# Two unused buffers in front of the h buffers and of the weight slots of a hybrid attention layer

## The reference

```python
x  = x + sincos_2d(rows, GRID_W, d)
m  = (silu(c) @ w_ada + b_ada).reshape(9, d)          # shift, scale, gate of each sub-layer; mc from c_ctx
# 1: half-step SwiGLU FFN (1024 -> 2*2816 -> 1024), latent and context
x  = LN(ALPHA * x  + 0.5 * gate * swiglu(modulate(LN0(x)),  ffn1_w_in, ffn1_w_out))
xc = LN(ALPHA * xc + 0.5 * gate * swiglu(modulate(LN0(xc)), ffn1_w_in, ffn1_w_out))
# 2: mixer: one input projection (1024 -> 4128), 4 GLA heads and 4 HGRN2 heads,
#    each a gated linear recurrence in both directions, started from the context's state;
#    head norm, gate, one output projection (1024 -> 1024), latent only
x  = LN(ALPHA * x + gate * mixer(modulate(LN0(x)), modulate(LN0(xc))))
# 3: a second half-step SwiGLU FFN, latent only
x  = LN(ALPHA * x + 0.5 * gate * swiglu(modulate(LN0(x)), ffn2_w_in, ffn2_w_out))
```

## The kernel before

| buffer | before | mod 512 |
|---|---|---|
| h_hi, h_lo | 16512, 41088 | 128, 128 |
| xl (the tokens), ident | 65664, 82048 | 128, 128 |
| c_cols (stationary of the modulation products) | 84352 | 384 |
| w_raw0, w_hi0, w_lo0 (and slot 1, 8192 further) | 90080, 106464, 122848 | 480 |
| half_hi0, half_lo0 (and slot 1, 8192 further) | 106464, 122848 | 480 |
| hid_hi, hid_lo (all stages) | 181216, 203744 | 480 |
| xn, hfull, glu, ada_block, vtok, attT, mT and the other working tiles | from 139232 | 480 |

## Time and profile before

### The profile page before, as it was taken

The page is one execution under the profiler, slowest core; times in us unless marked ns, Lnnn a source line. Parts: engine busy times, 40 slices in busy tenths (PEclk is TensorE's granted clock), DMA queues, the critical chain, the costliest instruction groups (busy, mean ns, idle before and its releaser), DMA issues.

```text
span 1559.1 us, 18192 instructions
## 1 busy us (share of the span) xinstructions
PE 1438.5 (92%) x7613; PEld 1164.3 (75%) x7613; DVE 711.1 (46%) x894; ACT 511.7 (33%) x697; POOL 81.7 (5%) x86
## 2 busy tenths in 40 slices
PE   5899999999999998999999999997748999999994
PEld 2677777777789998787777778886647887888783
DVE  4344323433336765453155456676663233332335
ACT  3234211222213555424253354553323222122220
POOL 3000000000000000000011011110000000000000
PEclk9899999999999999999999999998978999999997
DMA  9555456555435664450121112213322322433221
GB/s 290 185 154 157 144 180 188 164 162 155 156 108 136 172 180 122 152 186 17 42 67 41 27 28 55 55 55 135 108 54 79 111 90 86 109 82 107 75 74 54
DMA packets 201313, 177.06 MB, mean 114 GB/s; under 512 B 6522, under 2 KB 166792, under 8 KB 201232
## 3 DMA queue, kind: packets, MB, share of 16 engines
q1 hardware_dynamic: 191056, 137.97, 30.3%
q0 software_dynamic: 9856, 37.78, 7.2%
q10 hardware_dynamic: 320, 0.14, 0.0%
HBM read 173.78 MB, written 2.10 MB: 113 GB/s over the span
## 4 chain that ended last, share of the span: by engine, by line
PE 82%; DVE 7%; ACT 5%; issue 4%; DMA 1%; ACTq 0%; POOL 0%; DVEq 0%; POOLq 0%
PE ps L1563 25%; PE ps L1564 23%; PE ps L1565 23%; ACT w_hi L652 2%; PE ps L1587 2%; DVE w_lo L1044 1%; PE ps L1940 1%; PE ps L1938 1%; DVE stats L1059 1%; ACT hfull L671 1%; DVE xl L1096 1%; PE ps L1603 1%; PE ps L1923 1%; DVE xl L1089 1%; PE ps L1887 1%
## 5 line engine op out<-in xcount | busy, mean ns | idle before, releaser
L1044 DVE TENSOR_TENSOR w_lo<-w_raw,w_hi 128x2048 fp32r<-128x2048 f32 (+3 forms) x113 | 250.6, 2219 | 375.1 <-ACT w_hi L652 374.8
L1563 PE MATMUL ps<-h_hi,w_lo 128*128 128x512 f32 (+1 forms) x1104 | 397.9, 360 | 16.5 <-DVE h_lo L1082 10.8
L1564 PE MATMUL ps<-h_lo,w_hi 128*128 128x512 f32 (+1 forms) x1104 | 392.6, 356 | 0.0
L1565 PE MATMUL ps<-h_hi,w_hi 128*128 128x512 f32 (+1 forms) x1104 | 392.4, 355 | 0.0
L652 ACT ACTIVATE w_hi<-w_raw 128x2048 fp32r<-128x2048 f32 (+3 forms) x113 | 209.5, 1855 | 543.1 <-PE ps L1565 541.8
L1563 PEld LDWEIGHTS ps<-h_hi,w_lo 128*128 128x128 f32 x1104 | 210.4, 191 | 57.9 <-DVE h_lo L1082 11.6
L1565 PEld LDWEIGHTS ps<-h_hi,w_hi 128*128 128x128 f32 x1104 | 210.0, 190 | 32.3
L1564 PEld LDWEIGHTS ps<-h_lo,w_hi 128*128 128x128 f32 x1104 | 210.3, 190 | 30.3
L1563 PE MATMUL ps<-h_hi,half_lo 128*128 128x512 f32 (+1 forms) x272 | 103.8, 382 | 3.6 <-DVE gate L1407 3.3
L1564 PE MATMUL ps<-h_lo,half_hi 128*128 128x512 f32 (+1 forms) x272 | 99.8, 367 | 0.0
L1565 PE MATMUL ps<-h_hi,half_hi 128*128 128x512 f32 (+1 forms) x272 | 99.6, 366 | 0.0
(11 more groups left out here) (212 smaller groups left out, 1868.7 us busy)
## 6 DMA issues: line engine op xcount, KB each, us to landing
w_raw<-ffn_w_in SPq DMA_DIRECT2D x132, 512.0 KB, 5.2
ada_block<-w_ada POOLq DMA_DIRECT2D x36, 1024.0 KB, 5.9
w_raw<-ffn_w_out SPq DMA_DIRECT2D x60, 512.0 KB, 4.1
half_raw<-w_mix_in SPq DMA_DIRECT2D x48, 256.0 KB, 3.2
w_raw<-w_mix_out SPq DMA_DIRECT2D x12, 512.0 KB, 4.7
w_raw<-w_mix_in SPq DMA_DIRECT2D x8, 512.0 KB, 4.4
w_raw<-ffn_w_out SPq DMA_DIRECT2D x12, 256.0 KB, 3.8
xl<-x SPq DMA_DIRECT2D x4, 512.0 KB, 7.3
```

What stands on the lines that cost most here:

```text
L1044: nc.vector.tensor_tensor(lo, raw, hi.bitcast(F32), ALU.subtract).then_inc(s_lo[s], 1)
L1563: nc.tensor.matmul(dst, s_low, m_high, start=start, stop=False)
L1564: nc.tensor.matmul(dst, s_high, m_low, start=False, stop=False)
L1565: return nc.tensor.matmul(dst, s_high, m_high, start=False, stop=stop)
```

## The change

Two buffers that nothing reads or writes are allocated: `h_offset`, 88 floats a partition (352 bytes), in front of h_hi, and `w_offset`, 40 floats (160 bytes), in front of the weight slots. No instruction is added, removed or moved on any engine, and no wait; the operands' addresses alone differ. The source lines of the changed kernel are 1 higher from L158 on and 2 higher from L188 on.

```diff
@@ -155,6 +155,7 @@
             return ctx.enter_context(nc.semaphore(name))
 
 
+        sb("h_offset", [P, 88])
         h_hi = sb("h_hi", [P, KT, TOK], F32R)
         h_lo = sb("h_lo", [P, KT, TOK], F32R)
         xl = sb("xl", [P, TL, D])
@@ -184,6 +185,7 @@
         dec = [sb(f"dec{d}", [P, TL]) for d in range(2)]
 
 
+        sb("w_offset", [P, 40])
         with ExitStack() as s0:
             w_raw = [sb(f"w_raw{s}", [P, SLOT], F32, s0) for s in range(2)]
             w_hi = [sb(f"w_hi{s}", [P, SLOT], F32R, s0) for s in range(2)]
```

## The result

| | before | after |
|---|---|---|
| median of 4 runs each, us | 1562.84 (1561.61 to 1564.52) | 1546.3 (1545.0 to 1547.36) |
| profiled execution, us | 1560.92 | 1545.0 |
| span, us | 1559.1 | 1543.2 |

The ratio is 0.9893, 95% interval 0.9876 to 0.991: 16.5 us faster, where 22.1 were forecast. It lies inside the stated range.

The account below looks back on a forecast made before the run. TensorE's matmuls were taken to bound the kernel, most fully in both latent FFNs. Wide matmuls saving 17.7 us plus narrow ones saving 4.4 make 22.1, so the median goes from 1563.05 to 1541 us, range 1530 to 1555.

Parts of the forecast that it names:

- No change: Rival: something else about the h buffers (region, step, writing times) makes the spacings differ; saves 0, 1563 us; chance 0.09.
- Wide ones, 17.7 us: 512-column matmuls in L1, L2, heads, values, LR and output projection, mostly 7.6 or 6.0 ns faster each; 17.7 us together.
- a term for what an interruption costs: L1: matched matmuls run slow for 12 spacings behind an interruption, 2.4 us off 7.3, leaving 4.9.
- The values: 288 V matmuls with h stationary and w moving, 232.6 to 226.6 ns, saving 6.0 ns each, 1.7 us.
- the output projection: 192 matmuls at 6.0 ns save 1.2 us, half of it beside the norms that bound the stage: 0.6 counted.
- The first two blocks: L1's first 96 matmuls: nothing gained, as PE waits for DMA rows and runs partly at low clock; uncovered 0.7 us.
- Narrow ones, 4.4 us: 256-column matmuls in context FFN (2.9), heads (1.0), L2's pieces and LR: 118.5 to 114.2 ns, 4.4 us together.
- the matched excess: Time over 213.3 ns when both operands share a remainder: 13.3 ns for 512 columns, against 20.9 or 19.3 unmatched.
- The factor 0.65: Context FFN: share of narrow-matmul savings that counts, 113 us of products on the chain against 173 us run; 4.5 becomes 2.9.
- late next: After the change: nothing in L1 and L2; context FFN blocks go from 5.7 to 5.5 us, slot splits come nearer.
- Slower: Rival: h moving over w at equal remainders meets at every start, some 238 ns in FFN hidden blocks and heads; 1575 us; chance 0.06.
- Half: Rival: effect holds for one operand order only or only in unbroken stretches; saves 9 us, 1554; chance 0.06.

Follow-up runs that it names:

- w_alone: Only w_offset of the change: h stays at 128 modulo 512, weight slots and hid go to 128 too; 1544.73 us, 0.9882 of before.
- h_alone: Only h_offset of the change: h at 480, weight slots and hid at 320, so their distance stays 160; 1563.76 us, 1.0006 of before.
- the first sweep: Kernel of only matmul rows on zeros, layer left out, operand distance in 32-byte steps; 512 columns 226.7 ns at 0, 234.2 at 160.
- the third sweep: Matmul rows on zeros, layer left out: two operand pairs in turn, fewer stationary columns, two-byte elements; 230.0 ns with only next distances at 0.
- split160: Changed kernel with the context's part of h in its own buffers at distance 160, latent part at 0; 1546.0 us, 0.9898 of before.
- split112: Changed kernel with the context's part of h alone at distance 112 from the weight slots; 1542.23 us, 0.9869 of before.
- the second sweep: Matmul rows on zeros, layer left out, distance in 8-byte steps, plus other widths; 512 columns from 226.7 ns to 236.7 at distance 240.
- all240: Against the changed kernel, all of h moved to distance 240 from the weight slots; 1560.92 us, 0.9991 of before.
- all64: Against the changed kernel, all of h moved to distance 64 by the two offsets alone; 1551.8 us, 0.9934 of before.

## Why the prediction came out right, and where it did not

**The mechanism.** Equal remainders make the wide matmul 226.7 instead of 234.3 ns: shown, by the trace after, by w_alone and h_alone and by the first sweep. The modulus is 256; 512 is a multiple. That the moving operand meets the next stationary one is borne out in part by the third sweep (230.0 ns with the next distances at 0, 234.2 with the own ones). "No change" is refuted. The Trainium skill says in "TensorE: Matmul & The Clock Gate", Part 2, Step-by-step, that loading the next stationary operand takes no SBUF read bandwidth from the running matmul. For fp32r operands the measurement differs from what follows from that: placing alone moves the spacing from 234.3 to 226.7 ns; whether it is SBUF bandwidth that the two share, no run shows. For two-byte operands no run here contradicts the sentence. The same page of the Trainium skill, Weight-path perf modes, says that stationary operands of 128 columns are loaded in a faster way unless their type is FP32; whether that is why the two-byte ones know no distance, no run here shows.

**Wide ones, 17.7 us.** L1 was forecast at 4.9, with a term for what an interruption costs; its stretch from the first row turn to the last product is 4.5 shorter (382.37 to 377.90). L2's second part gave 4.06, with its output products, of 528 x 7.6 = 4.0. Its first part gave 1.8, but 2.8 to 2.9 in the three other profiles of kernels with the same spacings (162.41 before, 159.5 to 159.6 there). This profile has the clock at its lower level for one longer piece among the norms, here against before:

```profile
1122.40:1139.50 17.10, 7.74 (x35) 0.50 0.36 101
...
1134.10:1147.80 13.70, 6.22 (x28) 0.50 0.33 90
```

The three others have 13.7 us there too; split160 has 17 again, and 160.7 us. The values came at 6.7 ns a matmul where 6.0 were put; the output projection gave 0.9 where 0.6 was put. The first two blocks, at which I put nothing, gave 0.5: where the clock is up they are at 226.7 to 229 ns, not 234. Another 0.4 us of the table's first row lies ahead of the first wide product, where the change has no part.

**Narrow ones, 4.4 us: the failed step.** The prediction scaled the matched excess with the columns, "If it scales as in the wide ones (13.3 / 20.9 = 0.64 of 11.8), 114.2: a saving of 4.3. I take the last." The excess is 32 cycles at both widths, so 120.0, which was the upper bound. The 1056 blocks' matmuls lost 1.3 ns each, the heads' 240 2.2 (117.4 to 119.6 in the mean of unbroken spacings). On the path that is, as an estimate, some 1.5 us lost (0.7 in the context's stage, 0.5 in the heads, the rest in L2's pieces) instead of 4.4 gained. These 5.9 us are what lies between 22.1 and 16.5; that they come out at 5.6 so nearly is in part luck, since the other terms miss by up to 1.9 us both ways. split112 bears it out from the other side: it has the narrow ones at 113.5 and wins 3.5 us over the changed kernel.

The reason given, that the unmatched excess nearly scales with columns, was no ground for the matched one. A row for 256 columns at distance 0 was nowhere in the trace. The plain guess, that a settled pattern costs the same number of cycles at every width, would have been right at 256 columns; the second sweep shows that it is not a rule either (38 and 40 cycles at 448 and 480).

**The factor 0.65.** Of what a narrow matmul saves in the context FFN, split112 got 0.45, at an equal number of low-clock pieces. Its stage against the changed kernel's:

```profile
473.00:683.40 210.40, 197.74 (x1370) 184.29 (x1369) 127.67 (x135) 99.33 (x121) 0.00 (x0) 0.98 0.55 160
...
474.30:681.60 207.30, 191.47 (x1370) 178.13 (x1369) 127.63 (x135) 99.33 (x121) 0.00 (x0) 0.98 0.56 163
```

PE's busy time (the second number) fell by 6.3 us, the stage by 3.1, and PE's idle time rose from 12.7 to 15.8. Three kernels whose narrow matmuls save less against the changed kernel, also with two low-clock pieces and one profile each, got more of it: before 0.54 of 1.3 ns a matmul, all240 0.58 of 2.8, all64 0.59 of 2.2. So the share of the chain, 0.65, overstates it, and most in split112, whose blocks are the shortest. That fits blocks that meet the slot splits sooner, which was named as late next and left to the same factor; no run takes it apart further.

**The rivals.** "Slower" had its mechanism upside down: no kernel with distance 0 had a wide spacing over 230 in an unbroken stretch of 48 or more; in the hidden blocks, where it was to strike, the spacing is 226.7. "Half" did not occur.

**What stays open.** Why 256 bytes, which part of the memory or of TensorE is shared, what the own pair contributes, and which state the array is in when it enters a row. The sweeps and all240 show that there are such states, no run shows what they are.

## What to carry to other kernels

With fp32r operands at full clock, compare start-to-start spacings of matmuls of one shape; if they differ by 3%, look at the distance of moving and stationary operand modulo 256, and put those of 512 columns over 128 stationary ones at 0 by padding one buffer: one unused allocation was worth 1.2% here (w_alone). Plain fp32 was not measured. Other widths have other good distances, and these can differ between a sweep and a kernel; measure a width in the kernel itself, not only in a sweep. With two-byte operands there was nothing to win.

## What the runs showed of the hardware

- fp32r, 128 stationary and 512 moving columns: 226.7 ns at distance 0 modulo 256, 228.9 to 236.7 elsewhere in the sweeps (in all240 226.7 and 228.3 at distance 16); at the lower clock level 427 ns, the 512 columns alone, at distance 160 and in the kernel after, around 83 us, at distance 0.
- 128 stationary and 256 moving columns: 113.3 to 121.7 ns, 120.0 at distance 0; 384 columns took 173.3 at distance 0 and 176.7 at 96; 320 columns 146.7, 448 columns 200.0 or 202.7, 480 columns 216.7 or 218.3. 128 columns took 111.7 at each of eight distances and 192 columns the same 111.7 at three, so there it is not the moving columns that set the spacing.
- bf16, 128 stationary columns: 215.8 ns for 512 moving columns and 109.2 for 256, at all eight distances.
- Interrupted by a few short matmuls, a matched stream needs some 7 to 11 matmuls to settle again (11 behind the interruption of the earlier trace rows); in the timeline of before, h over w at distance 160 is back at its 234 with the second.
